# A fused decoder trunk on one core: token forms ahead of the norm, two units that share a last token tile, earlier weight sums, a norm sum of two products

## The reference, cut to what matters

```
def rms_norm(x, gain):
    y = x * rsqrt(mean(x * x, axis=-1) + 1e-6)
    return y * gain

def swiglu(x, w_gate, w_up, w_down):           # 1024 -> 2816 -> 1024
    return (silu(x @ w_gate) * (x @ w_up)) @ w_down

for layer in range(2):
    x = x + 0.5 * swiglu(rms_norm(x, g[0]), ...)
    x = x + mixer(rms_norm(x, g[1]), ...)      # even mixer, odd mixer
    x = x + 0.5 * swiglu(rms_norm(x, g[2]), ...)
```

## Time and profile before

| | |
|---|---|
| median of three runs | 2067.54 us |
| the profiled execution | 2063.33 us, with a span of 2061.5 us |
| TensorE busy | 1993.5 us, 97% of the span, 11150 matmuls |
| VectorE busy | 1362.0 us, 66% |
| ScalarE busy | 835.0 us, 41% |
| GpSimd busy | 489.1 us, 24% |
| granted TensorE clock, mean | 0.992 |
| chain that ended last | TensorE 83%, VectorE 10%, ScalarE 3% |

### The profile page before, as it was taken

The page is one execution under the profiler, slowest core; times in us unless marked ns, Lnnn a source line. Parts: engine busy times, 40 slices in busy tenths (PEclk is TensorE's granted clock), DMA queues, the critical chain, the costliest instruction groups (busy, mean ns, idle before and its releaser), DMA issues.

```text
span 2061.5 us, 27515 instructions
## 1 busy us (share of the span) xinstructions
PE 1993.5 (97%) x11150; PEld 1708.5 (83%) x11150; DVE 1362.0 (66%) x1746; ACT 835.0 (41%) x1194; POOL 489.1 (24%) x358
## 2 busy tenths in 40 slices
PE   8999999999989999998999999999998998999998
PEld 6888888876778999986899998777776787899997
DVE  5333333644578888867888886783467747888874
ACT  5323233425553433335334333454545334443332
POOL 1202111142322112222221122254024511211211
PEclk9999999999999999999999999999999999999999
DMA  4222223421223333232332323222200222323223
GB/s 174 96 99 98 97 92 135 141 82 45 69 67 108 103 103 103 93 93 72 113 100 95 112 94 105 85 86 86 74 1 1 72 97 80 109 95 112 96 90 102
DMA packets 61898, 189.25 MB, mean 92 GB/s; under 512 B 6096, under 2 KB 6352, under 8 KB 61776
## 3 DMA queue, kind: packets, MB, share of 16 engines
q1 hardware_dynamic: 61776, 187.52, 27.7%
HBM read 182.78 MB, written 4.72 MB: 91 GB/s over the span
## 4 chain that ended last, share of the span: by engine, by line
PE 83%; DVE 10%; ACT 3%; issue 1%; POOL 1%; DMA 1%; POOLq 0%; SPq 0%; DVEq 0%; ACTq 0%
PE BANKS L501 12%; PE BANKS L502 12%; PE BANKS L503 12%; PE BANKS L580 9%; PE BANKS L582 9%; PE BANKS L581 9%; PE BANKS L631 4%; PE BANKS L632 4%; PE BANKS L633 4%; DVE LO L1431 2%; PE BANKS L928 1%; ACT HI L1048 1%; PE BANKS L911 1%; PE BANKS L754 1%; DVE SQ L1785 1%
## 5 line engine op out<-in xcount | busy, mean ns | idle before, releaser
L1373 DVE TENSOR_TENSOR LO<-RING,HI 128x1024 fp32r<-128x1024 f32 (+1 forms) x136 | 174.7, 1285 | 351.1 <-ACT HI L990 351.0
L501 PE MATMUL BANKS<-XH,HI 128*128 128x512 f32 x880 | 349.4, 397 | 17.4 <-DVE XL L1381 17.3
L502 PE MATMUL BANKS<-XL,HI 128*128 128x512 f32 x880 | 344.3, 391 | 0.0
L503 PE MATMUL BANKS<-XH,LO 128*128 128x512 f32 x880 | 344.0, 391 | 0.0
L1932 POOL TENSOR_TENSOR TMP<-TMP,RSTD 128x512 f32<-128x512 f32 x66 | 98.4, 1490 | 653.9 <-ACT TMP L1070 653.9
L990 ACT ACTIVATE HI<-RING 128x1024 fp32r<-128x1024 f32 (+1 forms) x144 | 150.3, 1044 | 236.2 <-DMA RING<-gu_dram 95.8
L501 PEld LDWEIGHTS BANKS<-XH,HI 128*128 128x128 f32 x880 | 166.2, 189 | 59.8 <-DVE LO L1373 11.1
L580 PE MATMUL BANKS<-BF,ASH 128*128 128x256 f32 x684 | 195.3, 286 | 9.9 <-DVE ASL L1476 9.9
L502 PEld LDWEIGHTS BANKS<-XL,HI 128*128 128x128 f32 x880 | 166.4, 189 | 35.6 <-issue 1.9
L503 PEld LDWEIGHTS BANKS<-XH,LO 128*128 128x128 f32 x880 | 166.3, 189 | 34.9
L581 PE MATMUL BANKS<-BFL,ASH 128*128 128x256 f32 x684 | 194.2, 284 | 0.0
(11 more groups left out here) (250 smaller groups left out, 4751.4 us busy)
## 6 DMA issues: line engine op xcount, KB each, us to landing
RING<-gu_dram SPq DMA_DIRECT2D x176, 512.0 KB, 3.5
DRAW<-down_dram SPq DMA_DIRECT2D x48, 512.0 KB, 3.7
RING<-oin_dram SPq DMA_DIRECT2D x32, 512.0 KB, 3.4
RING<-down_dram SPq DMA_DIRECT2D x32, 384.0 KB, 3.1
RING<-down_dram SPq DMA_DIRECT2D x16, 512.0 KB, 3.4
RING<-ein_dram SPq DMA_DIRECT2D x16, 512.0 KB, 3.4
RING<-oout_dram SPq DMA_DIRECT2D x16, 512.0 KB, 3.5
RING<-eout_dram SPq DMA_DIRECT2D x8, 512.0 KB, 3.8
```

The costliest lines, as they stand in the source:

```text
L501: pe.matmul(PS[bank][:], HI[j][:, c], hi(k), start=(n == 0), stop=False)
L502: pe.matmul(PS[bank][:], HI[j][:, c], lo(k), start=False, stop=False)
L503: last = pe.matmul(PS[bank][:], LO[j][:, c], hi(k), start=False, stop=(n == len(order) - 1))
L1373: dve.tensor_tensor(LO[j][:, 0:kt * P], RAW[j][:, 0:kt * P], HI[j][:, 0:kt * P].bitcast(F32), ALU.subtract).then_inc(lo_ready, 1)
```

## The change

There are four edits.

1. The norm sum. SQ is split into a high part SQH (ScalarE, `squares_high`) and a low part SQL (VectorE, `squares_low`), and TensorE multiplies each by a column of ones that is broadcast (`one`, from SELR) in f32r. SELR is now made at the start. SQH and SQL lie where SG lies. In the even mixer, the odd mixer and at the start, the two operations stand directly in front of the norm (at the start in front of the split of unit 3); in the block FFNs inside the first six units.
2. All block FFNs and the odd mixer begin with `two_units`; the norm product follows both units. In FFN 0 it stood behind unit 1 already.
3. In the block FFNs the first six units have an order written out: forms 0, 1 and 2 and the splits of forms 0 and 1 stand ahead of the norm's root and reciprocal, which moved into this list; the sums for block 3 stand around up 1 instead of behind gate 2.
4. In blocks without an early part but with a next block (3 and 20) VectorE makes the next block's sums between the additions of this one, splits them before `whole_up` and `whole_gate`, and splits the right half of the gate weights before `up`.

```diff
+        SQH = at("SQH", [P, T], tmp0, 2 * TB, F32R)
+        SQL = at("SQL", [P, T], tmp0, 3 * TB, F32R)
...
             def norm(r):
+                one = SELR[:, HC:HC + 1].to_broadcast([P, P])
                 if r == 0:
-                    pe.wait_ge(cst_in, 16)
-                pe.wait_ge(sq_ready, 8 * r + 8)
-                pe.matmul(AUX[:], ones, SQ[:], start=True, stop=True).then_inc(norm_sum, 1)
+                    pe.wait_ge(sel_ready, 1)
+                pe.wait_ge(sq_lo, r + 1)
+                pe.matmul(AUX[:], one, SQH[:], start=True, stop=False)
+                pe.matmul(AUX[:], one, SQL[:], start=False, stop=True).then_inc(norm_sum, 1)
...
-                unit(q0, 0, KX, xh, xl, ready=x_tile_ready(r))
+                two_units(q0, x_tile_ready(r))
                 norm(r)
-                for n in range(1, 2 * PLAIN):
+                for n in range(2, 2 * PLAIN):
...
             def odd_mixer():
-                unit(q0, 0, KX, xh, xl, ready=x_tile_ready(4))
+                two_units(q0, x_tile_ready(4))
                 norm(4)
-                for j in range(1, SLOTS):
+                for j in range(2, SLOTS):
...
+            def squares_high(r):
+                act.wait_ge(sq_ready, 8 * r + 8)
+                act.activation(SQH[:], SQ[:], ACT.Copy).then_inc(sq_hi, 1)
...
# ScalarE, block FFN, in place of the loop over the six units
+                now = (2, 3, 5)[f - 1]
+                form_inputs(0)
+                squares_high(now)
+                form_inputs(1)
+                form_split(0)
+                form_inputs(2)
+                form_split(1)
+                norm(now)
+                split(4, whole)
+                form_inputs(3)
+                form_split(2)
+                split(5, whole)
+                silu(0, 1.0)
+                form_split(3)
+                h_high(0)
+                silu(1, 1.0)
+                split(6, whole)
+                h_high(1)
+                sums_split(PLAIN, 0)
+                sums_split(PLAIN, 1)
+                split(7, right)
+                silu(2, 1.0)
+                h_high(2)
...
+            def squares_low(r):
+                dve.wait_ge(sq_hi, r + 1)
+                dve.tensor_tensor(SQL[:], SQ[:], SQH[:].bitcast(F32), ALU.subtract).then_inc(sq_lo, 1)
...
# VectorE, block FFN, in place of the loop over the six units
+                form(0)
+                squares_low(now)
+                form(1)
+                form_split(0)
+                form(2)
+                form_split(1)
+                norm(now)
+                split(4, whole)
+                gate(0)
+                form(3)
+                form_split(2)
+                up(0)
+                split(5, whole)
+                gate(1)
+                form_split(3)
+                sums_first(PLAIN)
+                up(1)
+                sums_second(PLAIN)
+                sums_third(PLAIN)
+                dve.wait_ge(sum_made, 3 * block_count(f, PLAIN) + 3)
+                gate(2)
+                split(6, whole)
+                sums_split(PLAIN, 0)
                 sums_split(PLAIN, 1)
                 split(7, right)
+                up(2)
...
# VectorE, blocks 3 and 20
+                    elif nxt:
+                        mid_two(p)
+                        sums_first(nxt)
+                        mid_five(p)
+                        sums_second(nxt)
+                        sums_third(nxt)
+                        dve.wait_ge(sum_made, 3 * block_count(f, nxt) + 3)
+                        mid_three(p)
+                        split(2 * nxt, whole)
+                        sums_split(nxt, 0)
+                        whole_up(p)
+                        sums_split(nxt, 1)
+                        whole_gate(p)
+                        gate(p)
+                        split(2 * nxt + 1, right)
+                        up(p)
```

More of the change, by code:

```diff
@@ L271, in trunk @@
         xh_ready, xl_ready, sqt_ready, sq_ready = (sem(n) for n in ("xh_ready", "xl_ready", "sqt_ready", "sq_ready"))
+        sq_hi, sq_lo = sem("sq_hi"), sem("sq_lo")
         norm_sum, std_ready, rstd_ready = sem("norm_sum"), sem("std_ready"), sem("rstd_ready")
@@ L547, in ffn @@
                 unit(q0, 0, KX, xh, xl, ready=x_tile_ready(r))
-                if f:
-                    norm(r)
                 def quad(q, third, lq, last, first=0):
@@ L1083, in block_ffn @@
                 whole, right = slice(0, KMAX * P), slice(4 * P, KMAX * P)
-                for n in range(2 * PLAIN):
-                    p = n // 2
-                    if n % 2:
-                        h_high(p)
-                    else:
-                        silu(p, 1.0)
-                    if n + 4 < 2 * PLAIN:
-                        split(n + 4, whole)
-                    if n < 4:
-                        form_inputs(n)
-                    if 1 <= n <= 4:
-                        form_split(n - 1)
-                    if n == 4:
-                        split(6, whole)
-                        split(7, right)
-                        sums_split(PLAIN, 0)
-                        sums_split(PLAIN, 1)
+                now = (2, 3, 5)[f - 1]
[21 more added lines that the diff above has]
+                h_high(2)
                 for p in range(PLAIN, FT):
@@ L1227, in read @@
                     return r
-                act.wait_ge(cst_in, 16)
-                act.activation(SELR[:], CST[:, K_ROW:K_ROW + HC + 1], ACT.Copy).then_inc(sel_ready, 1)
                 for lq in range(8):
@@ L1342, in _ @@
                 square_tile(0, m)
+            act.wait_ge(cst_in, 16)
+            act.activation(SELR[:], CST[:, K_ROW:K_ROW + HC + 1], ACT.Copy).then_inc(sel_ready, 1)
+            squares_high(0)
             split_hi(0, 3, 8)
@@ L1348, in _ @@
             ffn(0, Q_FFN[0], 1, True)
+            squares_high(1)
             norm(1)
             even_mixer()
-            norm(2)
             block_ffn(1, Q_FFN[1], 3, True)
-            norm(3)
             block_ffn(2, Q_FFN[2], 4, True)
+            squares_high(4)
             norm(4)
             odd_mixer()
-            norm(5)
             block_ffn(3, Q_FFN[3], None, False)
@@ L1543, in block_ffn @@
                 whole, right = slice(0, KMAX * P), slice(4 * P, KMAX * P)
-                for n in range(2 * PLAIN):
-                    if n % 2:
-                        up(n // 2)
-                    else:
-                        gate(n // 2)
-                    if n + 4 < 2 * PLAIN:
-                        split(n + 4, whole)
-                    if n < 4:
-                        form(n)
-                    if 1 <= n <= 4:
-                        form_split(n - 1)
-                    if n == 4:
-                        sums_first(PLAIN)
-                        sums_second(PLAIN)
-                        sums_third(PLAIN)
-                        dve.wait_ge(sum_made, 3 * block_count(f, PLAIN) + 3)
-                        split(6, whole)
-                        sums_split(PLAIN, 0)
+                now = (2, 3, 5)[f - 1]
+                form(0)
[21 more added lines that the diff above has]
+                sums_split(PLAIN, 0)
                 sums_split(PLAIN, 1)
                 split(7, right)
+                up(2)
                 for p in range(PLAIN, FT):
@@ L1587, in block_ffn @@
                         mid_five(p)
[L1588 to L1591 removed]
+                        split(NU, slice(0, 6 * P))
                         mid_three(p)
[L1593 to L1599 removed]
+                        split(NU + 1, slice(0, 6 * P))
                         whole_up(p)
[L1601 to L1602 removed]
                         whole_gate(p)
                         gate(p)
[L1605 to L1608 removed]
+                        split(NU + 2, slice(0, 6 * P))
                         up(p)
[L1610 to L1611 removed]
                 split(NU + 3, slice(0, 6 * P))
@@ L1872, in _ @@
                     dve.tensor_copy(SQ[:], GT[:, 0, :]).then_inc(sq_ready, 1)
+            squares_low(0)
             split_lo(0, 3, 8)
@@ L1877, in _ @@
             ffn(0, Q_FFN[0], 1, True)
+            squares_low(1)
             norm(1)
             even_mixer()
-            norm(2)
             block_ffn(1, Q_FFN[1], 3, True)
-            norm(3)
             block_ffn(2, Q_FFN[2], 4, True)
+            squares_low(4)
             norm(4)
             odd_mixer()
-            norm(5)
             block_ffn(3, Q_FFN[3], None, False)
```

19 lines of the change are left out of this document (removed).

## The result

The changed kernel takes 2040.16 us (median of four runs, 2038.16 to 2041.75) where the one before took 2067.64 in the same series: ratio 0.9867, 95% interval [0.985, 0.9884], 27.5 us less. The forecast was 2029.0, 38.5 us less. In a later series the same two kernels had medians of 2040.77 and 2063.41 us, ratio 0.9889 [0.9869, 0.9909]: the changed kernel's time is the same, that of the kernel before is 4 us lower. The experiments ran in three series, in which the kernel before had medians of 2063.88 us (edits 4 and 2 alone, down weights first), 2062.72 us (the four from the small gate scaling to both cures) and 2063.41 us (the last three). The unaltered change was measured again only in the last, so where an experiment of the first two is set beside 2040.77 us, the ratios, each to the kernel before in its own series, are the firmer comparison.

What follows compares the result with a forecast made beforehand. TensorE was taken as the bound, busy 97% of 2061.5 us. Terms -2.8 - 4.3 - 3.4 - 17.1 - 6.0 - 4.9 = -38.5 us, off the 2067.5 us median, gave 2029.0 us; range 2022 to 2036.

Steps and rivals of the forecast that it cites:

- part 3: Block FFNs, forms ahead of the norm: weight-split waits entering block 3 fall from 18.4 to 1.3 us, -17.1; clock there, -6.0.
- signs of being wrong: TensorE waits several us for gate 0 or split 6, or its clock falls at a place where it was full.
- Norm sum (-2.8): Six norm sums as two single-pass products: -3.9 us of product time, +1.1 of new waits, together -2.8 us.
- Last tile (-4.3): Seams into second block FFN and odd mixer: waits of 2.91 and 2.85 us go, new waits 1.3 and 0.15.
- clock there (-3.4): Behind the same two seams the clock stays up, giving back 1.7 us each, -3.4 us.
- rival A: Block FFNs: contention on VectorE or ScalarE adds 3 to 4 us each; 10 us come back, 2039; chance 0.13.
- The clock: Full in five stretches: -3.4 us at two seams, -6.0 at three block 3 entries; no new loss booked.
- rival D: Low clock up to block 3; its full statement and size are missing from the text; chance 0.03.
- Blocks 3 and 20 (-4.9): Three waits of 1.64 us for split sums in block 21 go, -4.9 us; block 4 stays, 9.2 becoming 9.3.
- Rival B: Block 4's waits go too because VectorE arrives ahead: another -9 us, 2020; chance 0.08.
- Table loads: ScalarE's root and silu loads cost 1.28 us each in its busy stream, without the skill's further 1.38 us drain.
- Rival C: Block 3 really waits for late weights of unit 6; the 18.4 us and their clock stay, 2052; chance 0.05.

Runs made afterwards that it cites:

- down weights first: Changed kernel, with ScalarE and VectorE splitting the early down weights in block 4 ahead of the next block's weights and sums; 2029.92 us, ratio 0.9836.
- the small gate scaling: Changed kernel, with GpSimd scaling only 8 of 512 columns of the gates of pairs 0 to 2 in block FFNs, computation incomplete; 2025.76 us, ratio 0.9817.
- both cures: Changed kernel, with the first early down weights split first and VectorE scaling the gates of pairs 0 to 3; 2025.57 us, ratio 0.981.
- the last three: Changed kernel with eight unread products before block 4's early product, 2033.97 us; with edit 4 undone, 2043.78 us; and unaltered, 2040.77 us.

## Why the prediction was wrong

The direction held, and so did the account of the seams and of block 21; the sum was 13.3 us too large, and the median lies 4 us above the range of 2022 to 2036. Two steps failed: the durations that part 3 walked VectorE with, and the clock behind the new wait in block 4, booked at nothing. Two of the prediction's own signs of being wrong came true, a wait for split 6 (2.72 us) and a fall of the clock where it was full. Block 3 of the first block FFN starts 36.0 us after TensorE's first unit there (599.91 - 563.87) where 35 were forecast and 42 stood before; XL waits 11.4 us where 11.5 were forecast; LO, ASL and DLO together wait 14.5 us where I had under 3 and 8 to 10.

**1. Norm sum (-2.8): not confirmed.** The two products take 0.56 us in place of 1.12, a little more than the 0.46 I had. The waits for SQL are 0.31, 1.26 and 0.42 us where 1.0, 1.3 and none were walked. The 0.31 is luck: over the other profiles with this edit the first wait is 0.72 to 1.59 us. Undone, the time does not move by more than the intervals.

**2. Last tile (-4.3) and clock there (-3.4): right.** Both waits are gone, both seams run at 1.00. From the end of the second block FFN to the middle of the odd mixer the lead over the kernel before grows from 12.5 to 17.1 us, the 4.6 of 2.85 + 1.7. What I didn't say is that the edit alone makes the kernel before 7.2 us slower.

**3. Forms ahead (-17.1): the step that failed.** I wrote "split of unit 6 961.5 ... wait 0.4 ... two sum splits end at 963.8 ... wait 0.85", and "no wait" for the other two FFNs. With the 7.2 us of lead taken off, these are 954.3 and 956.6; they came at 957.2 and 960.5. Between gate 0 and the end of the sum splits the walk has 13.5 us; it took 17.3 (943.2 to 960.5), and the five stretched operations are 4.0 of it. The walk used paces of VectorE from operations most of which met none of GpSimd's, and put the first sums and both sum splits just where GpSimd scales a gate. That is the contention of rival A, which I gave 0.13: it "adds 3 to 4 us per block FFN" and "10 us come back: 2039". It added 4.0 in each block FFN, and 7.1 us of waits and 3.4 of clock came back at block 3, in the first and third FFN too, where I had written no wait (1.24 + 1.67 and 1.67 us). So rival A had this mechanism and its price right; the rest of the miss is the clock behind block 4.

**The clock (-3.4 booked in part 2, -6.0 in part 3, no loss at new places): failed at the new places.** The clock of the two seams and of the first and third entry came back. That of the second entry did not, because its wait was not 0.4 but 2.72 us. And I forecast "3.5 us of idle" ahead of the first early product and booked no clock behind it, although showed a fall behind each wait of 2.85 us. It was 2.04 us and fell three times of three. The bound that rival D went by, "waits up to 1.92 us left it full", held in that one profile and said nothing of what lies above, where the new waits fell; the 1.76 us with a fall in the change without edit 4 shows that it is no bound either. Waits of 2.59 us in the odd mixer with a low clock behind them stood in the prediction itself. That all three fell was in part luck: the same kernel profiled again fell behind one.

**4. Blocks 3 and 20 (-4.9): right for block 21,** and 1.5 us too cautious for block 4, where 7.8 us of waits stand for 9.3. Rival B, that they go altogether, did not happen. But VectorE was the bound there only in part: with the down weights split first the waits of block 4 are 4.0 us, so 3.8 of the 7.8 came from the place of that split in the list.

**5. Table loads: right.** They cost the 1.28 us of the earlier trace rows, with nothing behind them (ScalarE, after, second block FFN):

```profile
935.98 1.28 ACT L1013 ACT_TABLE_LOAD   x1
937.27 0.69 ACT L1013 ACTIVATE RSTD<-BANKS,EPST 128x512 f32<-128x512 f32 x1
```

935.98 + 1.28 is 937.26. The drain that the Trainium skill ("ScalarE: Activation LUTs", What ACT_TABLE_LOAD costs) adds to each switch is not in the rows.

Rival C (late weights) and rival D (low clock up to block 3) are out: in the block stages no operation of VectorE waits for a DMA, and units 2 to 5 run at 1.00 behind waits of 1.26 and 1.2 us.

**What stays open:** what decides the clock behind waits of 1.7 to 3 us, what edit 3 does alone (its share is read from the traces), and why the kernel before was 4 us faster in the later series while the changed one was not.

## What to carry to other kernels

When work of VectorE is moved, lay GpSimd's timeline beside the new place, and price each operation with both inputs in SBUF that overlaps with GpSimd at the stretched duration, not at that of the old place. When waits of several short kinds are merged into one longer wait, the sum of idle time may fall and the clock may still go: ask of each remaining wait how long it is in one piece, and book the clock behind it as a chance; one row without a fall does not show that the next one is free. Two parts of a change can have opposite signs alone and together, so test each with the other in place.

## What was not expected of the hardware

A wait of 2.04 us ahead of the same product lowered TensorE's clock in 11 of 18 cases, and in two profiles of one kernel in three and in one of three. With eight products that nobody reads, 1.8 us in an idle gap of 2.04, it was full in three of three. GpSimd's operation of 8 columns took 0.39 to 1.08 us and ended each time within 0.07 us of the end of the VectorE operation that it met.
